# An expert block loaded earlier into q, kk and v, other buffers moved to make room, and a reordered router, in a two-block transformer kernel

## What is computed

```python
h = x
mod = silu(c) @ w_ada + b_ada                  # 16 pieces "ada": 12 of w_ada, 4 of w_ada_f
sh1, sc1, ga1, sh2, sc2, ga2 = split(mod, 6)
u = modulate(rmsnorm(h, g_norm1), sh1, sc1)
y = hybrid_mixer(u, ...)                       # q, k, gt, a, r, v, gates; conv branch; gated linear attention; w_out
h = h + ga1 * y
u2 = modulate(rmsnorm(h, g_norm2), sh2, sc2)
y2 = hierarchical_moe(u2, ...)                 # router, 32 experts w1, w3, w2, two chosen per token
h = h + ga2 * y2
x = modulate(rmsnorm(h, g_final), shf, scf)    # shf, scf from w_ada_f
```

## Time and profile before

| what | value |
|---|---|
| median of 3 runs | 1441.7 us (1437.92 to 1446.5) |
| time of the profiled execution | 1443.55 us |
| its span | 1441.7 us |
| TensorE matmul busy | 1199.7 us (83%) |
| VectorE busy | 675.6 us (47%) |
| ScalarE busy | 449.9 us (31%) |
| read from memory | 372.03 MB, 261 GB/s over the span |
| mean granted TensorE clock | 0.92 of full speed |

### The profile page before, as it was taken

The page is one execution under the profiler, slowest core; times in us unless marked ns, Lnnn a source line. Parts: engine busy times, 40 slices in busy tenths (PEclk is TensorE's granted clock), DMA queues, the critical chain, the costliest instruction groups (busy, mean ns, idle before and its releaser), DMA issues.

```text
span 1441.7 us, 20119 instructions
## 1 busy us (share of the span) xinstructions
PE 1199.7 (83%) x8634; PEld 947.6 (66%) x8634; DVE 675.6 (47%) x1146; ACT 449.9 (31%) x643; POOL 2.2 (0%) x16
## 2 busy tenths in 40 slices
PE   5999998897865657555675599999998889899998
PEld 2789896686322223222231399899998889899986
DVE  2547987453200101101010464455657786678974
ACT  2543343442000000000000353343545454545453
POOL 0000000000000000000000000000000000000000
PEclk7799999999989879888788999899999999999999
DMA  9797862977999999999999565343443425345552
GB/s 355 253 317 241 278 165 89 360 253 304 420 420 420 420 420 418 420 421 420 420 420 415 201 213 183 108 133 118 148 161 116 142 93 193 115 158 182 190 203 88
DMA packets 169655, 374.48 MB, mean 260 GB/s; under 512 B 8263, under 2 KB 121305, under 8 KB 145881
## 3 DMA queue, kind: packets, MB, share of 16 engines
q1 hardware_dynamic: 167040, 369.55, 69.5%
q0 software_dynamic: 144, 3.54, 0.8%
q10 hardware_dynamic: 2376, 0.04, 0.1%
HBM read 372.03 MB, written 4.62 MB: 261 GB/s over the span
## 4 chain that ended last, share of the span: by engine, by line
PE 58%; DMA 21%; DVE 11%; SPq 5%; ACT 3%; issue 3%; DVEq 0%; ACTq 0%
PE bank L603 31%; DMA arena<-in_w 15%; PE bank L1231 4%; DVE arena L1262 4%; DMA above<-in_w 4%; PE bank L907 4%; SPq L2599 4%; DVE fine L1254 2%; PE bank L947 2%; ACT fine L2059 2%; DVE arena L1254 2%; PE bank L563 2%; PE bank L600 2%; PE bank L634 1%; DVE arena L1259 1%
## 5 line engine op out<-in xcount | busy, mean ns | idle before, releaser
L603 PE MATMUL bank<-fine 128*128 128x256 f32 x4512 | 564.6, 287 | 17.8 <-DVE fine L1254 17.7
L603 PEld LDWEIGHTS bank<-fine 128*128 128x128 f32 x4512 | 554.3, 195 | 31.9 <-issue 27.8
L1254 DVE TENSOR_TENSOR fine<-arena,fine 128x1024 fp32r<-128x1024 f32 (+2 forms) x263 | 299.6, 1168 | 181.5 <-ACT fine L2059 172.1
L2059 ACT ACTIVATE fine<-arena 128x1024 fp32r<-128x1024 f32 (+2 forms) x279 | 266.3, 984 | 197.5 <-PE bank L603 82.4
L2059 ACT ACTIVATE arena<-bank 128x256 f32<-128x256 f32 (+2 forms) x153 | 68.2, 473 | 523.9 <-PE bank L919 191.7
L907 PE MATMUL bank<-arena 128*32 128x512 f32 x640 | 121.6, 790 | 62.8 <-DMA arena<-in_w 41.2
L1254 DVE TENSOR_TENSOR arena<-arena,bank 128x512 f32<-128x512 f32 x8 | 8.4, 1052 | 286.7 <-PE bank L907 286.7
L907 PE MATMUL bank<-above,arena 128*32 128x512 f32 x384 | 75.1, 724 | 51.6 <-issue 21.6
L2059 ACT ACTIVATE arena<-arena 128x512 f32<-128x512 f32 (+6 forms) x90 | 61.1, 708 | 152.1 <-DVE arena L1262 62.2
L907 PEld LDWEIGHTS bank<-arena 128*32 128x32 f32 x640 | 30.4, 140 | 118.9 <-issue 117.3
L1262 DVE SCALAR_TENSOR_TENSOR arena<-arena 128x256 f32<-128x256 f32 (+3 forms) x262 | 107.7, 484 | 1.1 <-ACT arena L2059 0.8
(11 more groups left out here) (177 smaller groups left out, 784.5 us busy)
## 6 DMA issues: line engine op xcount, KB each, us to landing
arena<-in_w SPq DMA_DIRECT2D x118, 1024.0 KB, 26.8
above<-in_w SPq DMA_DIRECT2D x66, 1024.0 KB, 26.5
arena<-in_w_in SPq DMA_DIRECT2D x62, 1024.0 KB, 5.5
arena<-in_w_ada SPq DMA_DIRECT2D x24, 1024.0 KB, 9.8
arena<-in_ffn_w_up SPq DMA_DIRECT2D x22, 1024.0 KB, 5.1
arena<-in_ffn_w_down SPq DMA_DIRECT2D x11, 1024.0 KB, 5.0
arena<-in_w_ada_f SPq DMA_DIRECT2D x8, 1024.0 KB, 10.6
above<-in_w SPq DMA_DIRECT2D x12, 512.0 KB, 18.5
```

The lines of the kernel that those rows point to most:

```text
L603: ins = e.matmul(o, w[:, k, j * P:j * P + P], x[:, kt, :], start=start, stop=stop, skip_group_check=True)
L1254: return e.tensor_tensor(o, a, b, f)
L2059: return e.activation(o, i, f, bias=bias, scale=scale)
```

## The change

Five things change.

1. `wides` gets a fourth early buffer at `q_at` (the memory of `q`, `kk` and `v`) and loses the one over the third ring slot and the input. Block 3 is issued between `ada(14)` and `ada(15)`, behind the first two pieces of `w_out`. The number of buffers stays 8. So that the buffer at `q_at` can be a block's, the router's and experts' own buffers move: `uT` into the third ring slot, `ye` to the input's memory, others behind the block.
2. The three slots of the last ada halves are now the input's memory, `consts1` with `cacc`, and `u`. So half 25 waits for `act_on["conv"]` (before: for the attention output, as half 24) and half 26 for `x_lo_v["og", 1]` (before: for `act_on["conv"]`).
3. `oh` is loaded into `u` ahead of ada half 4, with its 33 rows in place of all 128, without a wait; its three products (L677 before) are made between `ada_sums(2)` and `ada_sums(3)`, and their copies by ScalarE and the write of the rows come earlier too.
4. The router: two `raw_logits` come ahead of the first sum of squares, `turn_h(0, 1)` ahead of the transposition of `rstd`. The count that the gather needs is made by 2 products in place of 3, and the other 2 come after the gather.
5. VectorE signals each scaled token tile of 4, and TensorE waits for each instead of for all 4.

```diff
-        oh = shaped(flat(v)[:, 0:1152], 3, 384)
+        oh = shaped(flat(u)[:, 0:1152], 3, 384)
...
-        ada_slots2 = [arena[:, q_at:q_at + SLOT], flat(v), arena[:, consts1_at:consts1_at + SLOT]]
+        ada_slots2 = [arena[:, xbase:xbase + SLOT], arena[:, consts1_at:consts1_at + SLOT], flat(u)]
...
-        uT_at = top[0]
-        uT = buf(2048, 2, 1024)
+        uT_at = 2 * SLOT
+        uT = buf(2048, 2, 1024, at=uT_at)
...
+        top[0] = q_at + WIDE
...
-        ye = buf(2048, 2, 1024)
+        ye = buf(2048, 2, 1024, at=xbase)
...
-        early = [arena[:, at:at + WIDE] for at in (early_at + WIDE, early_at + 2 * WIDE, early_at)]
-        wides = early + [arena[:, 0:WIDE]] + [above[:, WIDE * i:WIDE * i + WIDE] for i in range(FINE // WIDE)] + [
-            arena[:, WIDE:2 * WIDE]]
+        early = [arena[:, at:at + WIDE] for at in (early_at + WIDE, early_at + 2 * WIDE, early_at, q_at)]
+        wides = early + [arena[:, 0:WIDE]] + [above[:, WIDE * i:WIDE * i + WIDE] for i in range(FINE // WIDE)]
...
             ada_sums(2)
-            ada_sums(3)
-            ada_to_mod(0)
-            advance("q", 2)
...
                 e.matmul(bank[0:6, 0:384], rtab[0:33, 6 * g:6 * g + 6], oh[0:33, g, :], start=True,
                          stop=True).then_inc(*rep_made.up(g))
+            ada_sums(3)
+            ada_to_mod(0)
+            advance("q", 2)
...
-            e.wait_ge(*squares["most"])
-            e.matmul(bank[:, 0:256], ones, sq[:, 0, :], start=True, stop=False)
             e.wait_ge(*route["wr"])
             raw_logits(0)
             raw_logits(1)
+            e.wait_ge(*squares["most"])
+            e.matmul(bank[:, 0:256], ones, sq[:, 0, :], start=True, stop=False)
...
-            e.matmul(bank[:, 0:32], before, mask[:, 0, :], start=True, stop=True)
-            e.matmul(bank[:, 32:64], ones, mask[:, 0, :], start=True, stop=False)
-            e.matmul(bank[:, 32:64], before, mask[:, 1, :], start=False, stop=True)
-            e.matmul(bank[:, 64:96], ones, mask[:, 0, :], start=True, stop=False)
-            e.matmul(bank[:, 64:96], ones, mask[:, 1, :], start=False, stop=True).then_inc(*router.up("ranks"))
+            e.matmul(bank[:, 0:64], before, flat(mask), start=True, stop=False, skip_group_check=True)
+            e.matmul(bank[:, 32:64], ones, mask[:, 0, :], start=False, stop=True, skip_group_check=True).then_inc(*router.up("ranks"))
...
-                            e.wait_ge(*gathered[quad, th])
+
+                            e.wait_ge(*gathered[quad, th, 0])
                         for k in range(4):
+                            if wn == 0 and k:
+                                e.wait_ge(*gathered[(quad, th, k) if k < 3 else (quad, th)])
...
+                    elif f == 25:
+                        e.wait_ge(*act_on["conv"])
                     elif f == 26:
-                        e.wait_ge(*act_on["conv"])
+                        e.wait_ge(*x_lo_v["og", 1])
                     elif f >= 24:
                         e.wait_ge(*o_made[1, 1])
...
-                elif n < NW - 1:
+                else:
                     e.wait_ge(*products_of[PIECES1 - 1, 1])
-                else:
-                    e.wait_ge(*norm_sum[1])
...
             for j in range(4):
                 ada(j)
+                if j == 1:
+                    e.dma_start(flat(oh)[0:33, :], T["consts"][0:33, NCONST0 + NCONST1:NCONST]).then_inc(*oh_in.up(0, 16))
             load("q", 2)
-            e.wait_ge(*ada_sum[4])
-            e.dma_start(flat(v)[:, 0:1152], T["consts"][:, NCONST0 + NCONST1:NCONST]).then_inc(*oh_in.up(0, 16))
...
             load("w_out", 2)
+            expert(0, 3)
             ada(15)
             load("w_out", 2)
```

More of the change, by code:

```diff
@@ L283, in build @@
         cnt = buf(2)
-        uT_at = top[0]
-        uT = buf(2048, 2, 1024)
+        uT_at = 2 * SLOT
+        uT = buf(2048, 2, 1024, at=uT_at)
         hot = buf(2 * 32 * CAP, 2, 32, CAP)
         hot2 = hot.rearrange("p t e c -> p t (e c)")
+        assert top[0] <= q_at
+        top[0] = q_at + WIDE
         sendw = buf(512, 2, 2, 128)
@@ L298, in build @@
         combT = buf(256, at=xbase + 1024)
-        combB = buf(8192, 32, 256, at=uT_at + 2048)
-        assert uT_at + 2048 + 8192 <= moe_end
+        combB = buf(8192, 32, 256, at=q_at)
+        assert q_at + 8192 <= moe_end
         hidG = buf(2048, 2, 4, 256, at=uT_at)
@@ L419, in build @@
         ON_VECTOR = ("a", "gla_o", "w_out", "k2", "w_b", "w_c", "w_o")
-        early = [arena[:, at:at + WIDE] for at in (early_at + WIDE, early_at + 2 * WIDE, early_at)]
-        wides = early + [arena[:, 0:WIDE]] + [above[:, WIDE * i:WIDE * i + WIDE] for i in range(FINE // WIDE)] + [
-            arena[:, WIDE:2 * WIDE]]
-        assert 2 * WIDE == xbase + 2048
+        early = [arena[:, at:at + WIDE] for at in (early_at + WIDE, early_at + 2 * WIDE, early_at, q_at)]
+        wides = early + [arena[:, 0:WIDE]] + [above[:, WIDE * i:WIDE * i + WIDE] for i in range(FINE // WIDE)]
         NW = len(wides)
-        GENERAL = list(range(NW - 1))
+        GENERAL = [i for i in range(NW) if i != 3]
         NG = len(GENERAL)
@@ L851, in tensor_program @@
             turn_h(0, 0)
+            turn_h(0, 1)
             bank = misc(route_a, "rstd")
@@ L856, in tensor_program @@
             ins.then_inc(*router.up("rstd"))
-            turn_h(0, 1)
             bank = misc(route, "logits")
@@ L886, in tensor_program @@
             gather_tokens(0, (0,))
+            e.matmul(bank[:, 64:96], ones, mask[:, 0, :], start=True, stop=False, skip_group_check=True)
+            e.matmul(bank[:, 64:96], ones, mask[:, 1, :], start=False, stop=True, skip_group_check=True).then_inc(*router.up("count"))
             for quad in range(8):
@@ L1689, in gather_tokens @@
                         k = 4 * g + j
-                        ins = ts(xg[:, i, k, :], bank_of(gathered, (quad, g))[:, j * P:j * P + P], perm[:, 0, k:k + 1], ALU.mult,
-                                 perm[:, 1, k:k + 1], ALU.add)
-                    ins.then_inc(*gathered.up((quad, g)))
+                        ts(xg[:, i, k, :], bank_of(gathered, (quad, g))[:, j * P:j * P + P], perm[:, 0, k:k + 1], ALU.mult,
+                           perm[:, 1, k:k + 1], ALU.add).then_inc(*gathered.up((quad, g, j) if j < 3 else (quad, g)))
             e.wait_ge(*perm_in[0])
@@ L1710, in vector_program @@
             step(e.tensor_copy(rank, shaped(ranks[:, 0:64], 2, 32)))
+            e.wait_ge(*router["count"])
             step(e.reduce_max(cnt[:, 0:1], ranks[:, 64:96], AX), "count")
@@ L2177, in scalar_program @@
             norm_rows(0, lambda pair: h_in[1, pair // 2])
+            for g in range(3):
+                e.wait_ge(*rep_made[g])
+                act(rep[0:6, g, :], bank_of(rep_on, g)[0:6, 0:384], ACT.Copy).then_inc(*rep_on.up(g))
+            e.wait_ge(*rep_on[2])
+            e.dma_start(bass.AP(scratch.tensor, P * rows, [[384, 6], [6 * 384, 3], [1, 384]]), rep[0:6, :, :]).then_inc(
+                *row_out.up(0, 16))
             high_half()
@@ L2187, in scalar_program @@
             advance("q", 1)
-            for g in range(3):
-                e.wait_ge(*rep_made[g])
-                act(rep[0:6, g, :], bank_of(rep_on, g)[0:6, 0:384], ACT.Copy).then_inc(*rep_on.up(g))
-            e.wait_ge(*rep_on[2])
-            e.dma_start(bass.AP(scratch.tensor, P * rows, [[384, 6], [6 * 384, 3], [1, 384]]), rep[0:6, :, :]).then_inc(
-                *row_out.up(0, 16))
             e.wait_ge(*ada_sum[7])
```

## The result

| | kernel before | changed kernel |
|---|---|---|
| median of 15 runs each, same chip | 1443.85 us (1437.92 to 1446.86) | 1450.01 us (1444.88 to 1453.32) |
| profiled execution, its span | 1443.55, 1441.7 us | 1448.61, 1446.8 us |
| mean granted TensorE clock | 0.92 | 0.918 |

The ratio is 1.0042, with a 95% interval of 1.0028 to 1.0056: 6.1 us slower, between 4.0 and 8.1. The forecast was +5.8 us.

A forecast was written before the change was run, and what follows sets the result against it. The expert stage, at 417 GB/s, was taken to end a fixed time after block 8's issue, which waits for quad 0's first up products. Terms 8.9 + 2.6 - 3.8 - 1.9 = +5.8 us gave 1447.5 us, range 1440 to 1454.

The forecast's parts named there:

- The frame: Expert stage ends a fixed time after block 8's issue, which waits for quad 0's up products; an earlier block saves nothing.
- a growth of at least 1 us as a sign: Memory's idle gap before block 8 should become longer, not shorter, by 1 us or more.
- Term 1: Ada half 25 waits for the conv activation, holding back `pw` and everything behind it on SP: +8.9 us.
- I take the middle, 3.4: First `pw` piece lands 3.4 us behind half 25, between 2.7 and 4.1, at 263.8 us.
- Term 2: Block 3 queued ahead of halves 30 and 31 delays the `w_out` products: +2.6 us, with 0 to 1.7 more for clock.
- rival A: Half clock granted once more at the wait for halves 30 and 31: slower by more than 7.2 us; chance 0.30.
- Term 3: Router: raw products fill idle time, fewer count products and scalings stand on the path: -3.8 us.
- Term 4: Start: L677's products move between the sums of halves 5 and 6: -1.9 us, bounds 1.0 and 3.0.
- Free: New buffer places, finer waits of quads 1 to 7 and the flag count cost or gain nothing.
- B: Not slower: start gives 5.7 us and L811 loses no clock, +0.7 us, 1442.4 us; chance 0.16.
- C: Faster: wait for the conv activation is hidden and the block's 5.0 us earned, 1431 to 1436 us; chance 0.08.

The follow-up runs named there:

- slots_fixed: Changed kernel with halves 25 and 26 in memory of `q`, `kk`, `v`, halves 28 and 29 in `consts1` and `u`; block 3 still early: 1443.41 us, ratio 1.0008.
- start_router: Kernel before with parts 3, 4 and 5 of the change (start and router), old buffers and slots: 1436.76 us, ratio 0.9963.
- slots_fixed_late: As slots_fixed, but with block 3 issued behind the last `w_out` piece: 1436.07 us, ratio 0.9961 to the kernel before.
- wait_only: Kernel before with only the slots of halves 25 and 26 exchanged, so half 25 waits for the conv activation: 1449.27 us, ratio 1.0044.
- router_only: Kernel before with parts 4 and 5 of the change alone (the router): 1439.86 us, ratio 0.9981.
- block_late: Changed kernel with block 3 issued behind the last `w_out` piece, nothing else changed: 1441.96 us, ratio 1.0004 to the kernel before.
- block_only: Changed kernel with parts 3 to 5 undone, leaving early block 3 and the new slots: 1456.38 us, ratio 1.0094 to the kernel before.
- earlier_router: Kernel before with the shorter router and `oh` loaded after ada half 1, its products ahead of the sums of halves 4 and 5: 1437.33 us, ratio 0.9965.
- before_again2: Kernel before, no edit, profiled a third time: 1446.84 us, span 1445.0 us.

## Why the prediction was right, point by point

| term | forecast | timed: the pairs, mean | in the traces |
|---|---|---|---|
| 1, the wait that moved | +8.9 | 6.3, 4.9, 6.2: +5.8 | +7.1 |
| 2, block 3 in the queue | +2.6 (clock 0 to 1.7 more) | 5.5, 6.8, 7.2: +6.5 | +5.6 to +6.0; +2.5 against slots_fixed_late |
| 3, router | -3.8 | -2.7, -4.9, -2.5: -3.4 | -4.3 in the changed kernel |
| 4, start | -1.9 | -0.4, -2.6: -1.5 | hidden by the clock of the start |
| sum | +5.8 | +7.4; the change itself +6.1 | |

The sum of the pairs and the change itself agree within the intervals, which are over 2 us to either side for every pair.

**The frame held.** The stage ends a fixed time after block 8: from its issue to the last landing it was 444.9 us before and 445.3 after, at 417 and 416 GB/s. A block fetched early earns nothing that can be measured, as start_router and slots_fixed_late say. Where the 5.0 us went: the gap of the memory ahead of block 8 grew by 0.7 us (last landing 0.86 us ahead of the issue before, 1.59 after; 100 and 56 GB/s in the stretches), and the router took 4.3 of it. I had named a growth of at least 1 us as a sign, because I had the router at 3.8; this sign failed, by 0.3 us.

**Term 1 was too large.** The mechanism is as forecast: half 25 held for the conv activation, `pw` behind it, L812 started by "DMA arena<-in_w_conv_pw", memory idle at 2 GB/s in between. The failed step is "I take the middle, 3.4": the first `pw` piece landed 7.84 us after half 25's issue, not 8.7, 2.8 us behind half 25, which was the bound below. The Trainium skill ("DMA: Bandwidth & Descriptors", Anatomy of one DMA) gave 6.8 us as an estimate; that section is about transfers issued by GpSimd, and these two are issued by SP. The measured 7.84 lies between its figure and mine. With 7.84, L812 began 5.7 us later and not 6.6. The half clock cost it 1.8 us (15.88 against 14.05) and not 2.5. The landing of half 27 then came 7.6 us later and not 8.9 (counted from half 24's issue), and in wait_only 7.1 arrived at the end of `w_out`.

**Term 2 was too small, by more than its own margin.** The landing that I worked out, +2.6, is there: 3.2 us in the pair. Mis-sized is the clock, "0 to 1.7 more". It took 2.8 us in the changed kernel: the half clock covers half 31's sum and the first `w_out` products, and both lie on the path. That is rival A's mechanism. A did not come about in size, since term 1 was 7.1 us and A needs 8.6. So the forecast's +5.8 holds because 1.8 too much in the one and 3 too little in the other nearly cancel in the traces (by the timed pairs 3.1 and 3.9). That is luck: nothing in the working ties the two errors to each other.

**Term 3 was right to within a half of a microsecond.** Block 8 comes 20.3 us after the last `w_out` product (20.7 forecast, 24.5 before). The raw products begin right at its end (340.97). From there to the gather it was 15.6 us and is 12.1, 3.5 less where 2.95 were forecast; from gather to L911 5.23 became 4.42, the 0.8 that were forecast. The gather ran at half clock (L878 3.76 us, 0.50 between 353 and 357 us), as L880 did before. Not foreseen was the queue: in router_only four blocks wait for `w_out`, and 1.4 of the 4.9 us stay in their transfers. In the changed kernel three do, since there is a fourth early buffer, and the memory is idle again before block 8 (56 GB/s). So this buffer could earn up to 1.4 us, wherever block 3 stands. From the last `w_out` product to the last landing start_router needs 465.9 us, slots_fixed_late and the changed kernel 465.6, block_late 464.7, that is 0.3 to 1.2 us less; the timed 0.9961 and 0.9963 can't tell that from nothing.

**Term 4 was near the timed value, and is not to be read from the pair of traces.** Half 7's sum ends at 33.4 (33.5 forecast), and L564 is one row of 48. It ends at 46.1 (47.8 forecast). The +2.7 in the sums is there, and so is the 4.0 that leaves the path: what is left, with the clock, is small, as 1.5 us timed says. How much of that is order and how much is clock stays open, since each execution has its own clock there.

**Free.** block_late has all the new places and finer waits, and its segment, 97.6 us, is that of wait_only, 97.7, which has none of them. From block 8 to the last landing it takes 445.2 us, before 444.9.

**The rivals.** B needs the start at 5.7 us; measured is 1.5. C needs the wait hidden; wait_only excludes it, with an interval that begins at +3.5 us. What stays open is a loss behind the expert stage. From the last landing to the end the profile of before has 639.1 us and that of the changed kernel 640.2, but router_only has 646.1, start_router 642.7 and block_only 642.6, at a granted clock of 0.94 to 0.95 from 820 to 1240 us in place of 0.96. earlier_router, with the same router as the first two, has 639.2, and block_only has the old router. So the loss goes with a lower clock and is not bound to the new router; what brings it on is not shown. It is one reason why single profiles and timed values differ by a few microseconds.

## What to carry to other kernels

A wait in a queue costs what stands behind it, so the place of a wait matters more than the buffer it guards: the exchange of two slots alone was worth 6 us, and giving them memory that is free at once brought it back. Before a transfer is pulled forward, ask what the stage's end hangs on; here it was a product that frees a buffer, so the early block earned nothing that could be measured and pushed back two transfers that TensorE did wait for. A forecast whose total comes out can still have wrong terms; only kernels that carry one part each told them apart. And before two traces are subtracted at some position, profile the old kernel twice.

## What the runs showed of the hardware

- One kernel on one core ran 1437.5 and 1446.8 us, a spread of 0.6%. 6.0 us between two of its profiles come from the first 66 us: 4.4 from a granted clock of 0.54 against 0.77 between 20 and 50 us, and 1.4 from one of 0.79 against 1.00 between 58 and 66 us.
- In the changed kernel two waits of 1.4 and 1.7 us with one sum of 1.07 us between them were followed by a stretch at the lower clock level (0.52 from 316 to 323 us). All three kernels with the early block show it (in the changed kernel, slots_fixed and block_only, `w_out` products of 22.1 to 22.3 us in place of 20.4). It cost 2.8 us, nearly what the two waits took together. A single wait of 1.8 us at the same place (slots_fixed_late, before_again2) was followed by `w_out` products of 21.9 us, a loss of 1.5.
- A MiB that is issued alone took 5.1 us to land, and the next one behind it came 2.8 us later, while in the full stream one MiB takes 2.5.
